# State-space preparation divided anew between the engines, three scan buffers, and the norm sum one tile earlier

## The reference

```
dt = jnp.exp(log_dt)[:, None]
mag = jnp.exp(a_re * dt)
ab_re, ab_im = mag * jnp.cos(a_im * dt), mag * jnp.sin(a_im * dt)
den = a_re * a_re + a_im * a_im
f_re = ((ab_re - 1.0) * a_re + ab_im * a_im) / den
f_im = (ab_im * a_re - (ab_re - 1.0) * a_im) / den
bb_re = f_re[..., None] * b_re - f_im[..., None] * b_im
bb_im = f_re[..., None] * b_im + f_im[..., None] * b_re
# s_t = ab * s_(t-1) + bb u_t   (complex, 64 groups x 64 states, associative scan)
y = C_re s_re - C_im s_im + d * u
z = gelu(y) @ w_glu;  return z[..., :D] * sigmoid(z[..., D:])
```

## Time and profile before

| | us |
|---|---|
| median of 3 runs | 3163.5 (3162.32 to 3167.12) |
| profiled execution | 3166.94 |
| its span, first to last instruction | 3165.1 |
| TensorE matmul busy | 2860.0 (90%) |
| VectorE busy | 1655.8 (52%) |
| ScalarE busy | 1129.5 (36%) |
| GpSimd busy | 797.8 (25%) |
| mean granted TensorE clock | 0.947 |

### The profile page before, as it was taken

How to read it: one execution, slowest core, us unless ns; L and a number is a source line. 1 busy time by engine, 2 the same in 40 slices (tenths; PEclk the granted TensorE clock), 3 DMA queues, 4 the chain that set the end, 5 groups by cost and what they waited for, 6 DMA issues and landing times.

```text
span 3165.1 us, 33444 instructions
## 1 busy us (share of the span) xinstructions
PE 2860.0 (90%) x12734; PEld 2330.1 (74%) x12734; DVE 1655.8 (52%) x2089; ACT 1129.5 (36%) x1716; POOL 797.8 (25%) x627
## 2 busy tenths in 40 slices
PE   6898998999988989999997474799999999999998
PEld 4676887888766778778885364678887778878886
DVE  4587445334456964543433857455543457655533
ACT  4466333222335653332222133332232237522221
POOL 1354113213024631140313647012210003212200
PEclk9999999999989999999998666899999999999999
DMA  3110322223220112222222110222333220123232
GB/s 115 40 34 21 100 93 80 95 99 98 75 78 22 40 47 94 80 96 97 99 94 80 33 27 16 74 86 99 97 100 108 81 80 1 34 87 100 93 104 89
DMA packets 75602, 236.67 MB, mean 75 GB/s; under 512 B 9761, under 2 KB 18225, under 8 KB 75457
## 3 DMA queue, kind: packets, MB, share of 16 engines
q1 hardware_dynamic: 73856, 230.72, 22.1%
q0 software_dynamic: 896, 3.22, 0.3%
q10 hardware_dynamic: 704, 0.70, 0.1%
HBM read 228.31 MB, written 2.10 MB: 73 GB/s over the span
## 4 chain that ended last, share of the span: by engine, by line
PE 77%; DVE 11%; POOL 5%; ACT 4%; issue 2%; DMA 1%; SPq 1%; DVEq 0%; ACTq 0%; POOLq 0%
PE bank L1665 24%; PE bank L1667 24%; PE bank L1666 24%; PE bank L1947 2%; POOL FF L762 1%; DVE STAT L1378 1%; DVE S5S L1538 1%; POOL TMP L770 1%; PE bank L1814 1%; PE bank L1721 1%; DVE WL L1265 1%; POOL MKL L766 1%; PE bank L1853 1%; PE bank L1902 1%; DVE S5TD L1476 1%
## 5 line engine op out<-in xcount | busy, mean ns | idle before, releaser
L1265 DVE TENSOR_TENSOR WL<-RAWW,WH 128x1024 fp32r<-128x1024 f32 (+2 forms) x424 | 581.4, 1375 | 861.7 <-ACT WH L976 861.6
L1665 PE MATMUL bank<-UH,WH 128*128 128x512 f32 (+1 forms) x1920 | 769.5, 401 | 124.7 <-DVE WL L1265 54.8
L1666 PE MATMUL bank<-UL,WH 128*128 128x512 f32 (+1 forms) x1920 | 761.3, 396 | 0.0
L1667 PE MATMUL bank<-UH,WL 128*128 128x512 f32 (+1 forms) x1920 | 760.2, 396 | 0.0
L976 ACT ACTIVATE WH<-RAWW 128x1024 fp32r<-128x1024 f32 (+2 forms) x424 | 433.2, 1026 | 457.5 <-DMA RAWW<-weights 457.1
L1665 PEld LDWEIGHTS bank<-UH,WH 128*128 128x128 f32 (+1 forms) x1920 | 369.1, 192 | 219.7 <-issue 106.8
L1666 PEld LDWEIGHTS bank<-UL,WH 128*128 128x128 f32 (+1 forms) x1920 | 369.1, 192 | 78.8 <-issue 2.0
L1667 PEld LDWEIGHTS bank<-UH,WL 128*128 128x128 f32 (+1 forms) x1920 | 368.5, 192 | 79.3
L1665 PE MATMUL bank<-HH,WH 128*128 128x512 f32 x512 | 199.2, 389 | 0.0
L1666 PE MATMUL bank<-HL,WH 128*128 128x512 f32 x512 | 199.2, 389 | 0.0
L1667 PE MATMUL bank<-HH,WL 128*128 128x512 f32 x512 | 199.2, 389 | 0.0
(11 more groups left out here) (314 smaller groups left out, 4775.1 us busy)
## 6 DMA issues: line engine op xcount, KB each, us to landing
RAWW<-weights SPq DMA_DIRECT2D x424, 512.0 KB, 3.3
X<-x SPq DMA_DIRECT2D x8, 256.0 KB, 8.4
FF<-tables POOLq DMA_DIRECT2D x2, 1024.0 KB, 7.4
U<-S5U SPq DMA_DIRECT2D x16, 128.0 KB, 2.4
GEL<-U SPq DMA_DIRECT2D x128, 16.0 KB, 1.8
out<-FF SPq DMA_DIRECT2D x8, 256.0 KB, 2.5
S5B<-s_b POOLq DMA_DIRECT2D x1, 512.0 KB, 3.8
S5C<-s_c POOLq DMA_DIRECT2D x1, 512.0 KB, 4.6
```

What stands on the lines that cost most here:

```text
L1265: dve.tensor_tensor(slot_words(WL, c % SLOTS, size), slot_words(RAWW, c % SLOTS, size), f32(slot_words(WH, c % SLOTS, size)), ALU.subtract ...
L1665: nc.tensor.matmul(out_, w[0], x_[0], start=start, stop=False, **how)
L1666: nc.tensor.matmul(out_, w[0], x_[1], start=False, stop=False, **how)
L1667: return nc.tensor.matmul(out_, w[1], x_[0], start=False, stop=stop, **how)
```

## The change

1. **Poles first.** The exponential, sine, cosine and all steps up to the factors of B run at the kernel's start (`state_params` on GpSimd, 26 steps; ScalarE's share before and behind the first norm tiles; a reciprocal as VectorE's first instruction). Results go to a tile PA of their own. Their parameters come by a DMA of their own.
2. **Powers early.** GpSimd loads B, C and S5N and makes the powers as soon as the last attention layer's final norm factor is there, then the three memsets in the order S5M, S5CP, S5CT.
3. **B and C.** `s5_b` comes straight behind the sum tree, and with it ScalarE's negation and copies of C, which GpSimd and a later place did before. The powers `s5_power` stand behind evacuations 1, 3 and 4. The C side (`s5_c`) moves from GpSimd to VectorE, behind the steps of the turns; all 16 turned banks are emptied by ScalarE.
4. **Scan.** Three state buffers instead of two (the fifth part of a buffer becomes one shared tile S5X), one GELU buffer pair for each of the eight tiles instead of two in rotation.
5. **Norm sum.** `stat` stands in front of the fourth product and of the cut of its chunk, in all eight places, and one output tile more is evacuated behind the fourth product.

```diff
@@ linear
         for step in mm:
             step.lead = mm[:]
-        if early:
-            early()
         plan.add("tree", norm=norm)
+        if mid:
+            mid()
+        plan.add("stat", "g tot", norm=norm)
     for x in range(len(mm), len(jobs) + 1):
         if x < len(jobs):
             product(x)
             plan.cut_to(done_of(mm[x]) + 1)
...
-        if norm and x == LEAD:
-            plan.add("stat", "g tot", norm=norm)
-            if late:
-                late()
-        while evacuated < min(x, 1 + 2 * (x - LEAD) if norm else x):
+        while evacuated < min(x, 2 + 2 * (x - LEAD) if norm else x):
@@ plan_second
         plan.add("evac_u", "eu", m=x, j=mm.j, bank=mm.bank, done=mm.c)
-        if x == 0:
-            plan.add("s5_params3")
-            plan.add("s5_b")
-        if 2 <= x <= 4:
-            plan.add("s5_power", p=x - 1)
-        if x in (2, 4):
-            plan.add("s5_c", half=(x - 2) // 2)
-        if x in (5, 6):
-            plan.add(f"s5_grid{x - 5}")
+        if x in (1, 3, 4):
+            plan.add("s5_power", p=(x + 2) // 2 if x < 4 else 3)
+        if x in (6, 7):
+            plan.add(f"s5_grid{x - 6}")
...
     for f in range(2 * DT):
         plan.add("s5_turn", f=f)
+    for half in range(2):
+        plan.add("s5_c", half=half)
@@ GpSimd, second_block
-                    if st.kind == "s5_params0":
-                        pool.wait_ge(x_done.sem, x_done.room(2, DT - 1))
+                    if st.kind == "norm" and st.version == 0:
+                        pool.wait_ge(rstd.sem, rstd.after(LAYERS - 1, LAST_POST.g))
...
+                        pool.memset(S5M[:], 0.0).then_inc(zeroed.sem, 1)
+                        pool.wait_ge(x_done.sem, x_done.room(2, DT - 1))
+                        pool.memset(S5CP[:], 0.0).then_inc(zeroed.sem, 1)
+                        pool.memset(S5CT[:], 0.0).then_inc(zeroed.sem, 1)
@@ ScalarE, second
                 elif kind == "s5_b":
+                    act.wait_ge(s5_in, 48)
+                    act.wait_ge(zeroed.sem, 2)
+                    act.activation(S5C[:, 1], S5C[:, 1], copy, scale=-1.0).then_inc(sp_act.sem, 1)
...
-                elif kind == "s5_turn" and st.f % 2 == 0:
+                elif kind == "s5_turn":
@@ VectorE
+            dve.wait_ge(sp_pool.sem, 15)
+            dve.reciprocal(s5a(18), s5a(13)).then_inc(sp_dve.sem, 1)
             for k in range(DT):
                 dve.wait_ge(x_in[k], 16)
                 dve.sem_inc(x_done.sem, 1)
...
-                    else:
-                        dve.wait_ge(s5_sum.sem, s5_sum.after(2, st.m - 2))
+                    if st.m >= 3:
+                        dve.wait_ge(s5_sum.sem, s5_sum.after(2, st.m - 3))
@@ SyncE
-                    sp.wait_ge(ge_f.sem, ge_f.after(2, m - 2))
+                    sp.wait_ge(ge_a.sem, ge_a.after(2, 3 * (m - 2)))
@@ ScalarE and GpSimd, program start
+            act.wait_ge(sp_in.sem, 16)
+            act.activation(s5a(0), s5a(25), ACT.Exp).then_inc(sp_act.sem, 1)
+            act.wait_ge(sp_pool.sem, 2)
+            act.activation(s5a(7), s5a(1), ACT.Exp).then_inc(sp_act.sem, 1)
...
+            state_params()
```

More of the change, by code:

```diff
@@ L141, in linear @@
     norm, mm, evacuated = after.get("norm"), [], 0
-    early, late, ahead = (after.get(k) for k in ("early", "late", "ahead"))
+    mid, ahead = after.get("mid"), after.get("ahead")
     def product(x):
@@ L479 @@
 N_SECOND_PARAMS = S_A + 3 * PAIRS
+R_RE, R_IM, F_RE, F_IM, TURNS = range(5)
 MATS = ("ident", "ones", "ones_head", "rot_a", "rot_b", "neg_tri", "neg_ones", "mask")
@@ L785, in step @@
                                        ALU.subtract).then_inc(hid_l.sem, 1)
[L787 to L804 removed]
+            n = [0]
@@ L907, in second_block @@
                     elif st.kind == "s5_rot":
-                        a = [S5S[st.m % 2][:, k, :] for k in range(5)]
+                        a = [S5S[st.m % 3][:, k, :] for k in range(4)]
                         for k in (0, 2):
@@ L1142, in second @@
                                            ).then_inc(sp_act.sem, 1)
-                elif kind == "s5_c" and st.half == 0:
-                    act.wait_ge(sp_pool.sem, S5_NC)
-                    act.wait_ge(zeroed.sem, 3)
-                    for part in range(2):
-                        for g in range(2):
-                            rows = slice(HD * g, HD * g + HD)
-                            act.activation(S5CP[rows, part, :, GH * g:GH * g + GH], S5C[rows, part, :, :], copy
-                                           ).then_inc(sp_act.sem, 1)
                 elif kind == "s5_response":
                     act.preload_act_table_set(SIN_TANH)
-                elif kind == "s5_turn" and st.f % 2 == 0:
+                elif kind == "s5_turn":
+                    m, part = divmod(st.f, 2)
                     act.wait_ge(s5_tr.sem, s5_tr.after(2, st.f))
-                    act.activation(S5M[:, 0, 4 * (st.f // 2):4 * (st.f // 2) + 4].rearrange("p q j h -> p (q j h)"),
+                    act.activation(S5M[:, part, 4 * m:4 * m + 4].rearrange("p q j h -> p (q j h)"),
                                    BANK[2 + st.f % 4][:], copy).then_inc(tr_act.sem, 1)
@@ L1866, in second_pe @@
                     if st.f >= 4:
-                        tr = tr_dve if part else tr_act
-                        pe.wait_ge(tr.sem, tr.after(2, m - 2))
+                        pe.wait_ge(tr_act.sem, st.f - 3)
                     for q in range(4):
```

258 lines of the change are left out of this document (126 added, 132 removed).

## The result

The changed kernel takes **3107.5 us** (median of 4 runs, 3105.85 to 3112.14) against 3164.1 before (4 runs): ratio 0.9821, 95% interval 0.9809 to 0.9833. Forecast was 3107.3. Its profiled execution took 3105.85 us with a span of 3104.1 and a mean granted TensorE clock of 0.956; the two profiled executions differ by 61.0 us of span, a little more than the medians (56.6).

What follows compares the result with a forecast made beforehand. TensorE, the busiest engine, idles in the state-space layer, whose first part VectorE sets, slowed beside GpSimd. Terms -54.9 + 1.5 - 19.3 + 11 + 5.5 = -56.2 against the median 3163.5 gave 3107.3 us, range 3090 to 3127.

Steps and rivals of the forecast that it cites:

- State preparation: First part of the state-space layer: powers take 16 us instead of 44, so the response starts earlier, -54.9 us.
- The C side: 16 VectorE operations beside the response, 1.15 to 1.25 us each, covered by the response matmuls with 2 us to spare.
- the C side spills: Rival: C-side operations end at about 1805 instead of 1785, holding the first rotation 18 us: 3125 us. Chance 0.1.
- Turns: Behind the response: ScalarE empties all 16 banks alone, twelve at 0.53 instead of 0.44 us, +1.5 us.
- Loop and tail: Scan loop and last tile's GELU: third state buffer and per-tile GELU buffers remove waits, -19.3 us.
- Norm sum: Sum at the third tile in seven norm places besides the state-space one: longer idle and lower clock, +11 us.
- The convolution FFNs: Two norm places that win back 3.3 us of later TensorE waits; 0.9 us remains, 2 × 1.0 in all.
- Keys and values: Norm place already slow after its pause, with two mask copies between: the early sum costs 2.2 us.
- Start: Kernel's start: VectorE's first instruction waits for fifteen GpSimd steps and a fifth DMA, +5.5 us.
- The chunk behind the factor: Rival: in seven norm places the fourth product idles 12.08 us, each costing 11.7 us: 3178 us. Chance 0.03.
- The port as the only bound of the loop: Rival: the port VectorE and GpSimd share sets the scan loop, third buffer brings nothing: 3122.6 us. Chance 0.17.

Runs made afterwards that it cites:

- Experiment 8: Changed kernel with the C side's 16 operations back on GpSimd, directly behind its memsets: 3135.2 us, ratio 0.9912 to the kernel before.
- experiment 7: Changed kernel with the C side computed twice over on VectorE (20.3 us more work): 3120.6 us, ratio 0.9860 to the kernel before.
- Experiments 4 and 5: Changed kernel with, in 4, two state buffers instead of three: 3124.6 us; in 5, two GELU input buffers instead of eight: 3114.8 us.
- put back: Changed kernel with the norm sum again behind the fourth product, in every norm place except the state-space layer's: 3100.3 us, ratio 0.9789 to the kernel before.
- experiment 3: Changed kernel with the fourth product's weight chunk split ahead of the norm sum's factor, in eight places: 3080.3 us, ratio 0.9741 to the kernel before.
- experiment 2: Kernel before with only the early norm sum and first two evacuations earlier, except in the state-space layer: 3173.7 us, ratio 1.0032.
- experiment 6: Changed kernel with VectorE's reciprocal and its wait for fifteen GpSimd steps moved behind the eight input tiles: 3106.4 us, ratio 0.9809 to the kernel before.

## Why the prediction was right, point by point

That 3107.3 and 3107.5 differ by 0.2 us is luck: the four runs spread over 6 us, and in the profiled executions the seven stretches miss by up to 3.0 us each and by 4.8 in sum. What was right are the large term, to within a microsecond, the sizes of the others to within a few, and most of the waits behind them.

- **State preparation (-54.9, measured -54.0).** The fourth product starts 32.5 us after the norm's first lead product, against 31.1 before; the prediction had 31.6. The chain behind it is as walked: multiplies 2.5, writes 2.8, the three powers in one go. Experiment 8 shows the cause that the prediction named: give GpSimd the multiplies back and 27 us return. The other 27 were not tested singly: that they belong to the factor that is there in time, and to the parameter steps that no longer stand between, is argued from the traces, not shown. Part of it can be read there: in the kernel before TensorE stands idle 11.5 us for two evacuations into S5U, which need the factor (its waits of 1706 to 1842 us); the changed kernel's waits of 1706 to 1810 us have no such line.

```profile
PE bank L1665 <- DVE S5U L1455: 11.5, 2, 6.8
```

- **The C side.** A price of 1.15 to 1.25 was right (1.21 to 1.24), the cover was not: it is not the response with 2 us to spare. The C side ended at 1796.1, 0.4 us ahead of the turns, but nothing needed VectorE then: it waited another 13 us for ScalarE's table, and experiment 7 puts the spare at about 9. The rival "the C side spills" was therefore over-priced at 18 us.
- **Turns (+1.5, measured -0.6).** The mis-sized term. From the response to the turns it takes 26.2 us instead of 27.5; from the turns' start to the chunk inputs 10.0 instead of 9.8, though ScalarE empties all sixteen banks: its last thirteen copies take 6.47 us, 0.50 each, against TensorE's own 8.96 us for the sixteen, 0.56 each. The prediction had 0.53 a copy against 0.44 for TensorE. Why the response itself is 1.3 us shorter was not tested.
- **Loop and tail (-19.3, measured -17.7).** Back-rotations 11.9, 11.8, 12.9, 13.5, 14.2, 13.5 and 10.1 us apart, where the walk had 11.6, 11.6, 13.0, 13.7, 13.5, 13.4 and 10.2. Experiments 4 and 5 give each buffer its share: 12.8 us of the loop and 3.1 of the tail.
- **Norm sum (+11).** The profiled execution shows 5.2, the experiments 10 (put back) and 10 (alone, 6 to 14): the term stands. The mechanism stands too: idle 3.71 where 3.75 was worked out, and experiment 3 removes it with the chunk's place. The clock's 1.7 us a place is the lower of the two values seen, 1.6 and 3.0. The convolution FFNs are nearly even, as predicted: their seventh product is 1.3 to 2.8 us late (39.0 and 40.5 against 37.7), but by the ninth the waits won back leave +0.5 and -0.9. Keys and values pay 1.7 in the changed kernel's trace and 4.8 in experiment 2's, where 2.2 was predicted.
- **Start (+5.5, measured +6.2).** Right in size and, for the changed kernel, in cause: VectorE's wait. The fifth DMA's data was used at 11.06 where 10.1 was estimated. What I did not count are ScalarE's own two waits, hidden under VectorE's; alone they would hold 1.8 of it (experiment 6).
- **Rivals.** The chunk behind the factor would have had to cost 9.6 us a place; it cost 1.8 to 4.5 in the FFNs. The port as the only bound of the loop falls by the spacings, and by experiment 4, where the same work takes 15 us a tile for want of a buffer.

Beside GpSimd's memset, which reads nothing, VectorE's four multiplies with two inputs in SBUF took 2.49 us (1722.86, inside the memset's 1721.13 to 1728.07), beside its multiplies 8.7 to 10.3. The Trainium skill, "SBUF — State Buffer", section "Who interferes with whom", says that two SBUF inputs contend with a GpSimd instruction that reads SBUF, not with one that only writes it; by that rule the trace agrees. So the memsets may stand where, by experiment 8, the multiplies may not.

## What to carry to other kernels

When two engines share a stage, price each operation by whether the other engine reads at the same time: moving work to the engine that is already the bound can shorten the stage if it ends the company and the moved work lands where the engine is not needed (here under the response). Before moving a reduction earlier, look at what its consumer's queue holds behind it; here one weight chunk ahead of the factor turned a loss of 10 us into a gain of 15 to 20, both against the late sum. Follow a serial queue from its first late item: that nothing waits at its end does not say that the end is on time.

## What the runs showed of the hardware

- The same idle of 3.71 us of TensorE was followed by a granted clock of 0.62 over 4.1 us in one trace and 0.54 over 6.6 us in another. In the first, the three lead products ahead of it had taken 17.8 us, in the second 19.3. It is so at all 16 FFN places of the eight traces with this order: the sixth product stands at 35.1 to 35.2 us behind lead products of 17.7 to 17.8 us, and at 37.8 to 37.9 behind lead products of about 19.3. One profiled execution is not enough to price a place where the clock falls.
- The first three products of the program took 18.8 us to the norm sum in two traces, 20.5 in two and 21.0 to 21.5 in three others, all with the first product at 19.9 to 20.9 us. With the first product at 16.56 they took 20.5: part of the 4.4 us gained there is within what one execution differs from the next.
- The company of GpSimd is paid by VectorE's smaller operations with two inputs in SBUF too, not by the large multiplies alone: writes of 64 x 512 take up to 2.7 us each instead of 0.71, weight halves of 128 x 1024 2.4 to 3.3 instead of 1.2 (experiment 8), eight scans of 128 x 128 in the changed kernel's loop up to 7.8 instead of 3.8.
